# Attention values taken for four query tiles at once, one head later, in thirds behind the scores of the next head's rounds

## What is computed

```python
def block(qblk):
    s = jnp.einsum('bhgqd,bhkd->bhgqk', qblk, k_all).astype(jnp.float32) * scale
    pr = jax.nn.softmax(s, axis=-1).astype(v_all.dtype)
    return jnp.einsum('bhgqk,bhkd->bhgqd', pr, v_all)
```

## Time and profile before

| what | value |
|---|---|
| device time of three runs | 1763.65, 1761.56, 1763.86 us; median 1763.65 us |
| the profiled execution | 1760.44 us, its span 1758.7 us |
| PE busy, share of the span | 1646.6 us, 94% |
| PE weight loads | 1379.8 us, 78% |
| DVE busy | 1015.1 us, 58% |
| ACT busy | 559.0 us, 32% |
| mean granted PE clock | 0.966 of full speed |
| chain that ended last, share on PE | 82% |
| time from the first transpose of round 0 to the first matmul of the output projection | 1253.29 to 1334.69 us: 81.40 us |

### The profile page before, as it was taken

The page is one execution under the profiler, slowest core; times in us unless marked ns, Lnnn a source line. Parts: engine busy times, 40 slices in busy tenths (PEclk is TensorE's granted clock), DMA queues, the critical chain, the costliest instruction groups (busy, mean ns, idle before and its releaser), DMA issues.

```text
span 1758.7 us, 22097 instructions
## 1 busy us (share of the span) xinstructions
PE 1646.6 (94%) x8770; PEld 1379.8 (78%) x8770; DVE 1015.1 (58%) x1438; ACT 559.0 (32%) x880; POOL 65.2 (4%) x86
## 2 busy tenths in 40 slices
PE   6999998787899999999999999898899999999998
PEld 3688887575788887888888887787587878888886
DVE  2999993344574777367734445642884654344344
ACT  2313123554163231122320223631332643232233
POOL 0400000221000000000000000100000000000001
PEclk9999998698899999999999999898999999999999
DMA  9412212111512644345424132140001133233232
GB/s 293 149 45 72 72 48 84 43 55 39 153 36 91 212 151 168 108 145 202 143 84 155 49 96 60 37 147 25 24 1 49 49 96 120 73 98 117 73 99 92
DMA packets 134010, 169.45 MB, mean 96 GB/s; under 512 B 15970, under 2 KB 92450, under 8 KB 133930
## 3 DMA queue, kind: packets, MB, share of 16 engines
q1 hardware_dynamic: 133360, 168.11, 30.0%
q10 hardware_dynamic: 570, 0.22, 0.1%
HBM read 166.17 MB, written 2.15 MB: 96 GB/s over the span
## 4 chain that ended last, share of the span: by engine, by line
PE 82%; DVE 8%; ACT 4%; issue 2%; POOL 1%; DMA 1%; POOLq 0%; DVEq 0%; SPq 0%; ACTq 0%
PE acc L658 46%; PE acc L710 19%; PE acc L682 3%; PE acc L875 2%; PE acc L1048 2%; PE acc L1027 2%; PE acc L762 1%; DVE w_lo L1481 1%; PE acc L909 1%; PE acc L1002 1%; PE acc L630 1%; PE acc L853 1%; DVE x L1653 1%; DMA ada_w<-in_ada_w 1%; PE acc L888 1%
## 5 line engine op out<-in xcount | busy, mean ns | idle before, releaser
L658 PE MATMUL acc<-h_hi,w_hi 128*128 128x512 f32 (+1 forms) x1424 | 416.4, 354 | 6.8 <-DVE w_lo L1481 4.4
L658 PE MATMUL acc<-h_lo,w_hi 128*128 128x512 f32 (+1 forms) x1424 | 413.0, 351 | 0.0
L658 PE MATMUL acc<-h_hi,w_lo 128*128 128x512 f32 (+1 forms) x1424 | 412.4, 351 | 0.0
L1481 DVE TENSOR_TENSOR w_lo<-raw,w_hi 128x1024 fp32r<-128x1024 f32 x186 | 223.1, 1230 | 164.7 <-ACT w_hi L1066 164.6
L1066 ACT ACTIVATE w_hi<-raw 128x1024 fp32r<-128x1024 f32 x186 | 189.3, 1054 | 260.8 <-PE acc L710 225.0
L658 PEld LDWEIGHTS acc<-h_hi,w_hi 128*128 128x128 f32 x1424 | 230.5, 189 | 43.9 <-DVE w_lo L1481 4.8
L658 PEld LDWEIGHTS acc<-h_lo,w_hi 128*128 128x128 f32 x1424 | 231.3, 189 | 39.1
L658 PEld LDWEIGHTS acc<-h_hi,w_lo 128*128 128x128 f32 x1424 | 229.7, 188 | 38.4
L710 PE MATMUL acc<-w_hi,hid_hi 128*128 128x512 f32 x440 | 176.3, 401 | 0.0
L710 PE MATMUL acc<-w_lo,hid_hi 128*128 128x512 f32 x440 | 175.7, 399 | 0.0
L710 PE MATMUL acc<-w_hi,hid_lo 128*128 128x512 f32 x440 | 175.5, 399 | 0.0
(11 more groups left out here) (239 smaller groups left out, 2109.1 us busy)
## 6 DMA issues: line engine op xcount, KB each, us to landing
ada_w<-in_ada_w SPq DMA_DIRECT2D x88, 512.0 KB, 6.0
raw<-in_ffn_w_in SPq DMA_DIRECT2D x88, 512.0 KB, 3.6
raw<-in_ffn_w_out SPq DMA_DIRECT2D x44, 512.0 KB, 4.0
raw<-in_even_w_in SPq DMA_DIRECT2D x24, 512.0 KB, 4.5
ada<-in_ada_w SPq DMA_DIRECT2D x8, 1024.0 KB, 12.3
raw<-in_odd_w_in SPq DMA_DIRECT2D x12, 512.0 KB, 4.5
raw<-in_even_w_out SPq DMA_DIRECT2D x8, 512.0 KB, 4.6
ada_m<-in_ada_w SPq DMA_DIRECT2D x8, 512.0 KB, 4.0
```

The source lines that it names most:

```text
L658: last = nc.tensor.matmul(acc[:, s, m, t0:t1], w[:, slot, kk, c], x_[:, k, t0:t1], start=(k == 0 and q == 0), stop=(k == KD - 1 and q == 2))
L1481: return nc.vector.tensor_tensor(out_, in0, in1, op)
```

## The change

PE no longer takes the values of a round within that round. In rounds 0, 1 and 2 of each head from the second on, behind the scores, it takes a third of the values of the head before, for all 512 queries at once: two of the six key tiles (`attended`), each with 512 moving columns. Round 3 of a head takes no values. Of the last head the values are still taken tile by tile (`attended_tile`): tiles 0 and 1 in round 21, tile 2 in round 22 and tile 3 in round 23. `pT` grows from two places of one round to two places of one head (`[P, 6, 512]` each, in memory that earlier stages have used). `head_high` moves from i = 1 to i = 3, `head_low` from n % 4 == 2 to n % 4 == 0 two heads later, with the one of head 4 behind the loop, and `pv_done` counts heads instead of rounds. The copy into `pT` writes six pieces of 128 elements, 512 elements apart, instead of 768 in a row.

```diff
--- before.py
+++ after.py
@@ -303,7 +303,7 @@
         adiag = place("adiag", [P, 2, T], offset=A0 + 58240)
         rt1 = place("rt1", [P, 2, LAT], offset=A0 + 64384)
         ptile = place("ptile", [P, 2, T], offset=A0 + 68480)
-        pT = place("pT", [P, 2, T], offset=A0 + 74624)
+        pT = [place("pT0", [P, NT, LAT], offset=A0 + 28672), place("pT1", [P, NT, LAT], offset=A0 + 52096)]
         acol = place("acol", [P, 36], offset=ADA)
         arow = place("arow", [P, 24, 4], offset=ADA + 256)
 
@@ -1030,6 +1030,29 @@
 
             scores(0)
             scores(1)
+            def attended(hd, tiles):
+
+                if not tiles[0]:
+                    pe.wait_ge(sem("pT_ready"), NL * (hd + 1))
+                    if hd >= 2:
+                        pe.wait_ge(h_ready, KD + 2 + hd - 1)
+                for j in tiles:
+                    last = nc.tensor.matmul(bank(1, 1, hd % 2), v1[:, j, (hd // 3) * HD:(hd // 3 + 1) * HD], pT[hd % 2][:, j, :],
+                                            start=(j == 0), stop=(j == NT - 1))
+                if tiles[-1] == NT - 1:
+                    last.then_inc(sem("pv_done"), 1)
+
+            def attended_tile(i):
+
+                hd = N_Q - 1
+                pe.wait_ge(sem("pT_ready"), NL * hd + i + 1)
+                if not i:
+                    pe.wait_ge(h_ready, KD + 2 + hd - 1)
+                for j in range(NT):
+                    last = nc.tensor.matmul(bank(1, 1, hd % 2)[:, i * P:(i + 1) * P], v1[:, j, (hd // 3) * HD:(hd // 3 + 1) * HD],
+                                            pT[hd % 2][:, j, i * P:(i + 1) * P], start=(j == 0), stop=(j == NT - 1))
+                return last
+
             for n in range(N_Q * NL):
                 hd, i = divmod(n, NL)
                 pe.wait_ge(sem("pn_ready"), n + 1)
@@ -1040,15 +1063,12 @@
                 last.then_inc(sem("pT_full"), 1)
                 if n + 2 < N_Q * NL:
                     scores(n + 2)
-                pe.wait_ge(sem("pT_ready"), n + 1)
-                if hd >= 2 and i == 0:
-                    pe.wait_ge(h_ready, KD + 2 + hd - 1)
-                c = (hd % 2) * 512 + i * P
-                for j in range(NT):
-                    last = nc.tensor.matmul(acc[:, 1, 1, c:c + P], v1[:, j, (hd // 3) * HD:(hd // 3 + 1) * HD],
-                                            pT[:, n % 2, j * P:(j + 1) * P], start=(j == 0), stop=(j == NT - 1))
-                if n < N_Q * NL - 1:
-                    last.then_inc(sem("pv_done"), 1)
+                if hd and i < 3:
+                    attended(hd - 1, (2 * i, 2 * i + 1))
+                if hd == N_Q - 1 and i:
+                    if i == 1:
+                        attended_tile(0)
+                    last = attended_tile(i)
             last.then_inc(unit_done, 2)
             token_products(pe, "out1", h, lambda k: pe.wait_ge(h_ready, KD + k + 1))
             ffn(1, "out1", LAT)
@@ -1453,7 +1473,7 @@
             def head_high(hd):
 
                 if hd < N_Q - 1:
-                    act.wait_ge(sem("pv_done"), NL * (hd + 1))
+                    act.wait_ge(sem("pv_done"), hd + 1)
                 else:
                     psum_full(act, U["att"] + 1)
                 c = (hd % 2) * 512
@@ -1466,7 +1486,7 @@
                     act.wait_ge(sem("pT_full"), n - 1)
                 nc.scalar.activation(ptile[:, n % 2, :], acc[:, 0, n % 2, 0:T], ACT.Exp, bias=arow[:, n, 1:2],
                                      scale=acol[:, n:n + 1], accum_out=arow[:, n, 2:3]).then_inc(sem("score_exp"), 1)
-                if i_ == 1 and hd:
+                if i_ == 3 and hd:
                     head_high(hd - 1)
             head_high(N_Q - 1)
             edge("out1", 1, 3)
@@ -2058,17 +2078,20 @@
                 if n >= 1:
 
                     dve.wait_ge(sem("pT_full"), n)
-                    if n >= 3:
-                        dve.wait_ge(sem("pv_done"), n - 2)
-                    nc.vector.tensor_copy(pT[:, (n - 1) % 2, :], acc[:, 1, 0, 0:T]).then_inc(sem("pT_ready"), 1)
+                    hd, i = divmod(n - 1, NL)
+                    if hd >= 2 and not i:
+                        dve.wait_ge(sem("pv_done"), hd - 1)
+                    nc.vector.tensor_copy(pT[hd % 2][:, :, i * P:(i + 1) * P],
+                                          acc[:, 1, 0, 0:T].rearrange("p (j t) -> p j t", t=P)).then_inc(sem("pT_ready"), 1)
                 if n < N_Q * NL:
                     dve.wait_ge(sem("score_exp"), n + 1)
                     sd.done(nc.vector.reciprocal(arow[:, n, 3:4], arow[:, n, 2:3]))
                     sd.wait()
                     nc.vector.tensor_scalar(ptile[:, n % 2, :], ptile[:, n % 2, :], arow[:, n, 3:4], None, ALU.mult
                                             ).then_inc(sem("pn_ready"), 1)
-                    if n % NL == 2 and n > NL:
-                        head_low(n // NL - 1)
+                    if n % NL == 0 and n >= 2 * NL:
+                        head_low(n // NL - 2)
+            head_low(N_Q - 2)
             head_low(N_Q - 1)
             dve.wait_ge(h_ready, 2 * KD)
             nc.vector.tensor_copy(mark[:, 7:8], ident[:, 0:1]).then_inc(set_free[0], 1)
```

## The result

The changed kernel takes 1766.12 us (median of 11 runs, 1763.86 to 1770.76), the kernel before 1761.97 us (11 runs, 1757.11 to 1763.86). The ratio is 1.0029, with a 95% interval of 1.0018 to 1.0041: **slower by 0.29%**, some 5.1 us (3.2 to 7.2); the two medians lie 4.15 us apart. The forecast was slower by 5.8 us.

The account below looks back on a forecast made before the run. PE was taken to bound rounds at 3.31 us, just above a 3.08 us ring of DVE and ACT. Terms -0.92, +3.0 and +3.8 gave +5.9, taken as +5.8: 1763.65 + 5.8 = 1769.4 us, range 1765.3 to 1773.1.

Parts of the forecast that it names:

- this ring: DVE and ACT steps from maximum through exponential and scaling to the next maximum, once per attention round: 3.07 to 3.08 us.
- Narrow against wide: Value matmuls: 48 passes of 128 columns become 12 of 512 at 0.43 us each, saving 0.16 us a head.
- rival A: Wide value passes are cheap, about 0.2 us each, so the kernel is no slower: net -0.3 us, 1763.3 us; chance 7%.
- Head 0: Four attention rounds without values, each 3.08 us: 12.32 us against 13.24, 0.92 gained.
- Heads 1 to 4: Three rounds of 3.70 us and a round i = 3 of 2.88: 13.98 us a head against 13.24, 3.0 us lost.
- `head_low` in round i = 0: DVE's 0.60 us for it fits in the 0.6 us of slack under PE's 3.70 us round: no cost.
- Head 5: Rounds 20 to 22 of the attention take 3.70, 6.36 and 3.71 us: 13.77 against 9.93, 3.8 us lost.
- The copy in pieces: DVE's copy into `pT` in pieces of 128 elements takes 0.92 us against 0.96 in a row: no cost.
- The sum: Attention terms -0.92 + 3.0 + 3.8 give +5.9 us; a count by PE's idle time also gives 5.9; +5.8 taken.
- rival C: All DVE-bound attention rounds run at DVE's own 2.72 us instead: +3.7 us, 1767.4 us; chance 9%.
- Rival B, the clock: PE's idle time in the attention lowers its clock; one slow round of each kind costs 0.9 to 3.7 us; chance 12%.
- The 2.71 us ring: Transposes, copy, reciprocal, scaling, next transposes, tied by the single PSUM place; holds where a round's maximum and exponential are early.

Follow-up runs that it names:

- the short maximum: Maximum taken over 64 of 768 keys, scores multiplied by 0.05: in the kernel before 1759.75 us (ratio 0.9996), in the changed kernel 1763.89 us (1.0014).
- the kernel with four equal parts: Changed kernel with the previous head's values in four equal parts, one per round, instead of thirds: 1761.26 us, ratio 0.9998 to the kernel before.
- the kernel one round late: Kernel before, with each round taking the narrow values of the round before it and the last round taking both: 1759.71 us, ratio 0.9997.

## Why the prediction was right, point by point

- **What bounds the rounds.** Right. "PE's 3.31 us lies only 0.23 above this ring" is what decides. With the short maximum the kernel before stays at 3.31; the rounds of head 0, without values, fall to 3.08 and no further. Only "no round can fall much below 3.08 us" goes too far, by the prediction's own 2.88 for the rounds i = 3: behind longer rounds, in which DVE has got ahead, a short round took 2.79 us, and 2.72 in the kernel with all values in one round.
- **Narrow against wide.** Forecast 0.16 us a head, measured 0.18 with the thirds in narrow passes. Wide passes stand 0.43 us apart, so rival A falls. With it falls, for this float32 case, the ratio of the Trainium skill, "TensorE: Matmul & The Clock Gate", section "Back-to-back issue gap".
- **Head 0.** Forecast 12.32 us, measured 12.33.
- **Heads 1 to 4.** Forecast 13.98 us a head, measured 13.74 (13.72 in head 1): the term that was mis-sized, by 0.24 us four times. Two thirds of it are the rounds with a third, three of them at 3.60 to 3.68 instead of 3.70. The scores' 1.32 us held part of the wait for the copy, 0.16 us in the earlier trace rows; where nothing waits, transposes, scores and a third take 0.66, 1.29 and 1.71 us by the starts of their matmuls (round 6, 1273.24 to 1276.90), 3.66 in all. The other part is the round i = 3, counted as 2.88.

That second part can be read in the timeline of DVE and ACT around the end of head 1:

```profile
1277.11 0.60 ACT L1480 ACTIVATE h_hi<-acc 128x512 fp32r<-128x512 f32 x1 [2.76 <-PE acc L1040]
1277.60 0.98 ACT L1487 ACTIVATE ptile<-acc,arow,acol 128x768 f32<-128x768 f32 x1
...
1277.76 0.96 DVE L2084 COPY pT<-acc 128x768 f32<-128x768 f32 x1 [0.86 <-PE acc L762]
1278.71 0.16 DVE L2088 RECIPROCAL arow<-arow 128x1 f32<-128x1 f32 x1
```

`head_high` waits for the third third and then holds the next exponential back, as forecast. But that one starts 0.49 us behind it, not 0.60, and so the reciprocal comes 0.95 us after the copy where 0.88 is the least: the delay is 0.07 us, not 0.17 (5.73 - 5.55 is 0.18 by the prediction's own figures). From the transposes of round 7, 0.97 us ahead of their copy (1276.79), to those of round 8 (1279.58) it is 2.79 us.

- **`head_low` in round i = 0.** Forecast as free because of 0.6 us of slack; it used up the slack and little more. PE's load for round 9 waited for DVE: round 8 took 3.68 us, where round 4, the first with a third and without `head_low`, took 3.60.
- **Head 5.** Forecast 13.77 us for rounds 20 to 22, measured 13.68. The wait in round 22 is covered, the one in round 23 stays at 1.29:

```profile
1334.48 0.69 PEld L762 LDWEIGHTS acc<-ident,ptile 128*128 128x128 f32 x6
1336.46 1.42 PEld L1052 LDWEIGHTS acc<-pT,v 128*128 128x128 f32 x12 [1.29 <-DVE pT L2084]
```

- **The copy in pieces.** 0.95 to 0.96 us, as before: nothing.
- **The sum.** Forecast +5.8 us (both of its counts give 5.9, and nothing is named for the 0.1), the trace gives 86.20 - 81.40 = +4.8, the runs +5.1 (3.2 to 7.2). The 1.0 us between forecast and trace is heads 1 to 4. The predicted 1769.4 us lies 3.3 above the measured median. About half of that (1763.65 - 1761.97 = 1.7) is the kernel before: two of the three runs that the forecast started from are the highest of the eleven. The other half is the sum (5.8 against the 4.15 between the two medians). The measured 1766.12 us lies 0.8 above the lower end of the range, and that end was set by rival C, which did not come. So the time alone says little for the prediction; the rounds do.
- **Rival B, the clock.** In no trace here did the granted clock leave 1.00 between 1262 and 1330 us, although PE stood idle about a microsecond at a time. It was low in rounds 0 and 1 of five of the nine traces, at a cost of 0.2 to 1.2 us (last section), but in neither of the two traces that are compared above. The swinging that the Trainium skill, "TensorE: Matmul & The Clock Gate", section "A second HAM failure mode: psum-queue depth-cycling", describes is not seen between 1262 and 1330 us.
- **Rival C.** The 2.71 us ring is real (2.65 with the short maximum) but holds head 0 only where the maximum is short; with the full one, ACT's exponential comes too late, and 3.08 holds.

## What to carry to other kernels

Before work of the bounding engine is moved to other rounds, work out for each round how long that engine holds it and how long the next ring of the other engines takes. A busy share of 100% says nothing of how near that ring is; here it was 7% away, so taking all values out gave back only 0.23 us in each round of head 0, and 0.5 to 0.6 in one that stands behind a longer round, while what was added to another round counted in full. Work that is put off by a whole head leaves the first head short of it and the last one with more: in equal shares that came to some 0.5 us by the trace. Put off by one round, in equal shares, it cost nothing and covered a wait.

## What the runs showed of the hardware that was not expected

**The first rounds run at either clock, from one execution to the next.** Ahead of round 0 PE waits for DVE for 1.2 us or more, in all kernels. In the trace of before and in that of the changed kernel the granted clock was 1.00 from 1253 us on. In the kernel with four equal parts it was at the low level in the same place, though it is the same as the changed kernel up to there:

```profile
1253.00:1256.00 3.00, 2.73 (x8) 2.01 (x9) 2.41 (x6) 1.08 (x2) 0.00 (x0) 0.50 0.03 11
1256.00:1259.00 3.00, 3.00 (x10) 2.18 (x9) 2.02 (x4) 0.35 (x1) 0.00 (x0) 0.50 0.00 0
```

This cost 1.2 us; in the second trace of the changed kernel it cost 0.2, in the kernel one round late about 0.7, in that with narrow thirds 0.55, in that with all values in one round 0.9. These five are all kernels that take no values in round 0, but in each of them the clock fell before PE had come to the place where the values of round 0 used to stand. In the second trace of the changed kernel the transposes of round 0 begin at 1251.20 us at full clock and the scores at 1251.91, and the clock falls while these run:

```profile
1252.00:1253.00 1.00, 1.00 (x3) 0.35 (x2) 0.96 (x3) 0.71 (x1) 0.00 (x0) 0.71 0.00 0
1253.00:1254.00 1.00, 1.00 (x3) 0.34 (x1) 0.68 (x3) 0.38 (x2) 0.00 (x0) 0.50 0.00 0
```

So the missing values did not bring it down; whether they make the low clock last or cost more is not tested. The cost is as large as the effects of some experiments, so a comparison of stretches has to look at the clock of rounds 0 and 1 first.

**Short idles did not bring the clock down there.** Head 0 of the changed kernel has four idle pieces of 1.3 us between weight loads (0.9 between its busy records), one in every 3.08 us, and stayed at 1.00 (the windows row of head 0 above).
